# The FFN's first product of a two-layer decoder turned round: tokens as the stationary operand, 32x32 turns on VectorE, transfers within SBUF

## The reference, cut to what matters

```python
D_MODEL, SEQ, DEPTH, CONV_WIDTH = 1024, 256, 2, 3
D_FF = 2816

def conv_ffn(x, w_in, conv_w, conv_b, w_out):     # x (1, 256, 1024), w_in (1024, 5632), w_out (2816, 1024)
    up, gate = jnp.split(x @ w_in, 2, axis=-1)
    up = lax.conv_general_dilated(                 # per feature, over this token and the two before it
        up, conv_w[:, None, :], window_strides=(1,), padding=[(CONV_WIDTH - 1, 0)],
        dimension_numbers=("NWC", "WIO", "NWC"), feature_group_count=up.shape[-1]) + conv_b
    return (jax.nn.gelu(up) * gate) @ w_out

x = layer_norm(DEEPNORM_ALPHA * x + conv_ffn(x, ...), g, b)
```

## Time and profile before

| | us |
|---|---|
| median of three runs | 600.32 (600.27 to 600.74) |
| span of the profiled execution | 598.3 |
| PE busy | 589.4 (99%) |
| DVE busy | 464.9 (78%) |
| ACT busy | 323.7 (54%) |
| POOL busy | 50.5 (8%) |

### The profile page before, as it was taken

How to read it: one execution, slowest core, us unless ns; L and a number is a source line. 1 busy time by engine, 2 the same in 40 slices (tenths; PEclk the granted TensorE clock), 3 DMA queues, 4 the chain that set the end, 5 groups by cost and what they waited for, 6 DMA issues and landing times.

```text
span 598.3 us, 8585 instructions
## 1 busy us (share of the span) xinstructions
PE 589.4 (99%) x3216; PEld 501.1 (84%) x3216; DVE 464.9 (78%) x841; ACT 323.7 (54%) x520; POOL 50.5 (8%) x84
## 2 busy tenths in 40 slices
PE   8999999999999999999999999999999999999995
PEld 6887777898888888889888888889888888888894
DVE  4989994877777778777979797688677777777776
ACT  5756684265445444456445678935554555545430
POOL 6300000300000000000120003132000000000003
PEclk9999999999999999999999999999999999999998
DMA  8996865363556686554457955343755555755601
GB/s 306 296 341 215 261 186 189 139 223 109 184 191 209 211 280 211 192 169 173 172 203 222 302 177 186 108 140 101 251 191 182 188 170 204 242 172 201 210 2 70
DMA packets 82293, 116.38 MB, mean 195 GB/s; under 512 B 11292, under 2 KB 60236, under 8 KB 82252
## 3 DMA queue, kind: packets, MB, share of 16 engines
q1 hardware_dynamic: 80812, 111.64, 56.3%
q0 software_dynamic: 1152, 4.19, 2.1%
q10 hardware_dynamic: 288, 0.00, 0.0%
HBM read 108.23 MB, written 1.05 MB: 183 GB/s over the span
## 4 chain that ended last, share of the span: by engine, by line
PE 98%; DVE 1%; ACT 0%; DVEq 0%; issue 0%
PE wide L1294 18%; PE wide L1295 18%; PE wide L1296 18%; PE score L1501 11%; PE score L1507 6%; PE turn L1501 5%; PE outb L1501 5%; PE outb L1507 3%; PE turn L1507 3%; PE score L1307 1%; PE turn L1393 1%; PE outb L1419 1%; PE score L1296 1%; PE score L1295 1%; PE score L1294 1%; PE wide L1315 1%
## 5 line engine op out<-in xcount | busy, mean ns | idle before, releaser
L965 DVE TENSOR_TENSOR w_lo<-raw,w_hi 128x2048 fp32r<-128x2048 f32 (+1 forms) x120 | 211.0, 1776 | 60.6 <-ACT w_hi L772 60.4
L772 ACT ACTIVATE w_hi<-raw 128x2048 fp32r<-128x2048 f32 (+1 forms) x126 | 182.2, 1483 | 34.5 <-PE wide L1296 23.6
L1294 PE MATMUL wide<-w_hi,xT 128*128 128x512 f32 (+1 forms) x256 | 95.7, 374 | 0.3 <-DVE w_lo L1031 0.2
L1294 PE MATMUL wide<-w_hi,oT_hi 128*128 128x512 f32 x240 | 95.3, 397 | 0.0
L1295 PE MATMUL wide<-w_lo,oT_hi 128*128 128x512 f32 x240 | 93.7, 391 | 0.0
L1296 PE MATMUL wide<-w_hi,oT_lo 128*128 128x512 f32 x240 | 93.6, 390 | 0.0
L1296 PE MATMUL wide<-w_hi,xT 128*128 128x512 f32 (+1 forms) x256 | 93.0, 363 | 0.0
L1295 PE MATMUL wide<-w_lo,xT 128*128 128x512 f32 (+1 forms) x256 | 92.9, 363 | 0.0
L893 ACT ACTIVATE qT<-kT,conv_cols 128x256 f32<-128x256 f32 x36 | 21.7, 602 | 93.1 <-DVE kT L1198 93.1
L1501 PE MATMUL score<-xT,w_hi 128*128 128x512 f32 x288 | 68.3, 389 | 0.0
L1501 PEld LDWEIGHTS score<-xT,w_hi 128*128 128x128 f32 x288 | 53.9, 188 | 11.1
(11 more groups left out here) (182 smaller groups left out, 809.6 us busy)
## 6 DMA issues: line engine op xcount, KB each, us to landing
raw<-in_ffn_w_in SPq DMA_DIRECT2D x44, 1024.0 KB, 5.1
raw<-in_ffn_w_out SPq DMA_DIRECT2D x22, 1024.0 KB, 4.9
raw<-in_a_w_qkv SPq DMA_DIRECT2D x9, 1024.0 KB, 6.1
raw<-in_w_kv_shared SPq DMA_DIRECT2D x8, 1024.0 KB, 5.6
raw<-in_a_w_o SPq DMA_DIRECT2D x4, 1024.0 KB, 6.5
raw<-in_b_w_q SPq DMA_DIRECT2D x4, 1024.0 KB, 5.1
raw<-in_b_w_o SPq DMA_DIRECT2D x4, 1024.0 KB, 5.1
raw<-in_a_w_qkv SPq DMA_DIRECT2D x4, 512.0 KB, 7.7
```

The lines of the kernel that those rows point to most:

```text
L772: ins = nc.scalar.activation(w_hi[c % RING][:, part], raw[c % RAW_RING][:, part], ACT.Copy)
L965: ins = nc.vector.tensor_tensor(w_lo[c % RING][:, part], raw[c % RAW_RING][:, part], w_hi[c % RING][:, part].bitcast(F32), ALU.subtract)
L1294: nc.tensor.matmul(dst, a_hi, b_hi, start=start, stop=False, skip_group_check=True)
```

## The change

The first product holds the tokens stationary in every group: x's high or low part for 128 tokens is loaded, and 512 columns of weights stream past, 256 of `up` and 256 of `gate`. A chunk of `w_in` is now four of the eight row blocks for both, loaded by two transfers. The result has tokens on partitions, in two PSUM banks per group (`in_banks`, two pairs in turn). DVE turns each bank by blocks of 32x32 into `turned` (`turn_in`), SP moves the blocks in four transfers to `in_moved` (`in_move`), which is a part of the tensor `kT`, and ACT copies `up` out of it and applies the middle tap (`taps`). What was added up, copied or turned by TensorE is gone. The second product runs two groups behind, and the hidden tiles have four buffers. The splits of chunks are written ahead of the instructions that wait for a move.

```diff
+HIDDEN = 4
+MOVE_AHEAD = 6
...
         if which == 2:
-            return base + 3 * i + 2 if i == GROUPS - 1 else base + 3 * i + 4
-        return base + 3 * i - 1 + which if i > 0 else base + which
+            return base + (3 * i + 6 if i < GROUPS - 2 else 2 * GROUPS + i)
+        return base + (2 * i if i < 3 else 3 * i - 2) + which
+
+    def second_behind(i):
+
+        return [i - 2] if i >= 2 else []
...
+    for layer in range(LAYERS):
+        for i in range(GROUPS):
+            ffn_moves_ahead[ffn_chunk(layer, i, 1) + MOVE_AHEAD] = (layer, i)
...
+            def in_move(layer, i):
+                t = GROUPS * layer + i
+                sp.wait_ge(in_turned, ST * t + ST)
+                for a in range(4):
+                    sp.dma_start(in_moved[:, a, :], turned[32 * a:32 * a + 32, t % 2, :, :]).then_inc(in_carried, 16)
-            def load(c, dst, src):
+            def load(c, *parts):
+                if c in ffn_moves_ahead:
+                    in_move(*ffn_moves_ahead[c])
...
+                def taps(i):
+
+                    t = GROUPS * layer + i
+                    act.wait_ge(in_carried, 64 * (t + 1))
                     for tt in range(2):
+                        if t > 0:
+                            act.wait_ge(conv_done, 2 * t + tt - 1)
+                        nc.scalar.activation(by_quarters(up[:, tt, :]), carried(tt), ACT.Copy)
+                        nc.scalar.activation(by_quarters(conv[:, tt, :]), carried(tt), ACT.Identity,
...
+                for i in range(GROUPS):
+                    split_hi(ffn_chunk(layer, i, 0) + RING)
+                    if i:
+                        make_h_hi(i - 1)
+                    if i < GROUPS - 1:
+                        split_hi(ffn_chunk(layer, i, 1) + RING)
+                        for n in second_behind(i):
+                            split_hi(ffn_chunk(layer, n, 2) + RING)
+                        taps(i)
+                        make_gelu(i)
+                    else:
+                        split_hi(ffn_chunk(layer, i, 1) + RING, 0)
+                        split_hi(ffn_chunk(layer, i, 1) + RING, 1)
+                        taps(i)
+                        make_gelu(i)
+                        make_h_hi(i)
...
+                def turn_in(i, st):
+
+                    t = GROUPS * layer + i
+                    dve.wait_ge(*((in_rows_done, t + 1) if st == 0 else (chunk_used, ffn_chunk(layer, i, 1) + 1)))
+                    if st == 0 and t >= 2:
+                        dve.wait_ge(in_carried, 64 * (t - 1))
+                    bank = (wide[0:2] if i == 0 else in_banks[(i - 1) % 2])[st]
+                    into = turned[:, t % 2, :, :].rearrange("p b (j s t) -> p b j s t", j=4, s=ST)
+                    nc.vector.transpose(into[:, :, :, st, :], bank[:, :].rearrange("p (j f b) -> p b j f", j=4, b=4)
+                                        ).then_inc(in_turned, 1)
...
+                for i in range(GROUPS):
+                    turn_in(i, 0)
+                    split_lo(ffn_chunk(layer, i, 0) + RING)
+                    turn_in(i, 1)
+                    if i:
+                        for tt in range(2):
+                            make_h_lo(i - 1, tt)
+                    if i < GROUPS - 1:
+                        split_lo(ffn_chunk(layer, i, 1) + RING)
+                        for n in second_behind(i):
+                            split_lo(ffn_chunk(layer, n, 2) + RING)
+                        add_taps(i)
+                        for tt in range(2):
+                            make_hidden(i, tt)
+                    else:
+                        split_lo(ffn_chunk(layer, i, 1) + RING, 0)
+                        split_lo(ffn_chunk(layer, i, 1) + RING, 1)
+                        add_taps(i)
+                        for tt in range(2):
+                            make_hidden(i, tt)
+                            make_h_lo(i, tt)
...
+                def in_product(i):
+
+                    t = GROUPS * layer + i
+                    chunks = [ffn_chunk(layer, i, h) for h in range(2)]
+                    banks = wide[0:2] if i == 0 else in_banks[(i - 1) % 2]
+                    if i >= 3:
+                        pe.wait_ge(in_turned, ST * (t - 2) + ST)
+                    for h, st in ((0, 0), (1, 0), (0, 1), (1, 1)) if i == 0 else ((0, 0), (0, 1), (1, 0), (1, 1)):
+                        c = chunks[h]
+                        for k in range(4):
+                            kt = 4 * h + k
...
+                            if i == 0 and st == 0 and kt in (6, 7):
+                                x_transposes(2 * layer + 1, (kt - 4,))
...
+                            last = product(banks[st][:, :], xT_hi[:, kt, rs], xT_lo[:, kt, rs],
                                            w_hi[c % RING][:, cols], w_lo[c % RING][:, cols], kt == 0, kt == KT - 1)
...
+                for i in range(GROUPS):
+                    in_product(i)
+                    for n in second_behind(i):
                         for st in range(ST):
                             for half in range(2):
-                                last = second_product(ffn_chunk(layer, i - 1, 2) % RING, 0, st, half, start=second)
+                                last = out_product(n, st, half)
                         last.then_inc(chunk_used, 1)
```

More of the change, by code:

```diff
@@ L349, in ffn_chunk, with raw_count @@
         if which == 2:
-            return base + 3 * i + 2 if i == GROUPS - 1 else base + 3 * i + 4
-        return base + 3 * i - 1 + which if i > 0 else base + which
[L353 to L362, removed]
+            return base + (3 * i + 6 if i < GROUPS - 2 else 2 * GROUPS + i)
+        return base + (2 * i if i < 3 else 3 * i - 2) + which
+    def second_behind(i):
+        return [i - 2] if i >= 2 else []
+    IN_CHUNKS = {ffn_chunk(layer, i, h) for layer in range(LAYERS) for i in range(GROUPS) for h in range(2)}
+    def raw_count(c):
+        return sum(32 if n in IN_CHUNKS else 16 for n in range(c % RAW_RING, c + 1, RAW_RING))
+    ffn_moves_ahead = {}
+    for layer in range(LAYERS):
+        for i in range(GROUPS):
+            ffn_moves_ahead[ffn_chunk(layer, i, 1) + MOVE_AHEAD] = (layer, i)
     moves_ahead = {}
@@ L582, in load @@
                 slot = c % RAW_RING
[L583 removed]
+                for into, src in parts:
+                    sp.dma_start(into(raw[slot][:, :]), src).then_inc(raw_in[slot], 16)
             for layer in range(LAYERS):
@@ L915, in ffn_group, with make_h_hi @@
[L915 to L924, removed]
-                ffn_group(GROUPS - 1, "last")
+                def make_h_hi(i):
+                    for tt in range(2):
+                        act.wait_ge(hidden_done, 2 * (GROUPS * layer + i) + tt + 1)
+                        if tt == 0 and i >= HIDDEN:
+                            act.wait_ge(chunk_used, ffn_chunk(layer, i - HIDDEN, 2) + 1)
+                        nc.scalar.activation(hT_hi[i % HIDDEN][:, tt, :], hidden[:, tt, :], ACT.Copy).then_inc(hhi_done, 1)
@@ L1243, in ffn_group @@
-                    if peeled == "last":
-                        make_hidden(0)
-                        split_lo(cu + RING, 1)
-                        make_h_lo(0)
-                        make_hidden(1)
-                        make_h_lo(1)
-                        if cg + RING == SHARED:
-                            split_shared_lo()
-                        return
-                    for tt in range(2):
-                        make_hidden(tt)
-                    if not first:
-                        split_lo(cg + RING)
@@ L1604, in _ @@
                         x_transposes(2 * layer + 2, (0,))
-                    last = second_product(ffn_chunk(layer, i, 2) % RING, int(final), st, half, stop=final)
+                    last = out_product(i, st, half)
                     if (st, half) == (1, 1):
```

287 lines of the change are left out of this document (73 added, 214 removed).

## The result

The changed kernel takes 601.92 us (median of 11 runs, 600.56 to 603.21) against 600.25 (11 runs, 599.84 to 601.01): ratio 1.0029, 95% interval 1.0019 to 1.0038. It is slower by about 1.7 us, where 599.1 was predicted. The time lies inside the range that was given (597.2 to 604.0), on the side of the first rival (601.8 for a fall of the clock in one layer).

What follows compares the result with a forecast made beforehand. TensorE's matmuls were taken to bound the kernel. Per layer 12.4 + 152.4 + 11.3 = 176.1 us against 176.7, 1.2 less in both, so 600.3 - 1.2 = 599.1 us; range 597.2 to 604.0.

Steps and rivals of the forecast that it cites:

- the first rival: Clock falls to 1.2 GHz in the wait before group 10's second product: 601.8 us in one layer, 604.5 both; chance 0.25.
- The price of 0.0130 per start: TensorE's matmuls: each costs 0.0130 us beside its columns, so 256 columns take 0.1199 and 512 take 0.2268.
- Group 0: Start of each layer's FFN: 12.4 us, with TensorE waiting 0.6 for the norm's half row.
- The chain behind T: After T, the end of group 10's first product: turn, moves, copies, taps and low parts take 11.3 us per layer.
- PE's wait: TensorE stands still before group 10's second product, 11.3 - 8.2 = 3.1 us in each layer.
- the unknown costs: Bounds per layer: slower PSUM turns add 0.7 to 1.4, a landing at 6.2 adds 3.5, copies -0.2 to 0.4.
- a wait of about 3 us at full clock, 0.58: Likeliest case, at each layer's end: no clock fall, 599.1 us, bounds 597.7 to 600.4; chance 0.58.
- the stretch: From the FFN's first matmul to group 10's second product: 176.1 us predicted against 176.7 before, per layer.
- The price of a fall: Group 10's second product after a clock fall: 12 matmuls at double price, 2.7 us per layer.
- Late landings: Rival: moves land late at the layer's end or inside groups; 602.5 us, at 6.2 it is 606; chance 0.09.
- A shorter chain: Rival: steps at the layer's end overlap better, wait 1 us shorter per layer, 597.1 us; chance 0.06.
- The gain itself: Whole kernel at full clock: 0.6 us less per layer, 1.2 us in both.

Runs made afterwards that it cites:

- halves: The changed kernel with every 512-column matmul of the first product made as two of 256, output not the reference's; 616.15 us.
- hid: The changed kernel with both of DVE's products with the gate made before the low parts in group 10; 600.00 us.
- cover: The changed kernel with group 7's second product moved behind group 10's first product; 594.90 us.
- fill12: The changed kernel with twelve unused 512-column matmuls in TensorE's wait before group 10's second product; 599.40 us.
- fill6: The changed kernel with six unused 512-column matmuls in TensorE's wait before group 10's second product; 599.14 us.
- cover2: Cover with the next layer's first chunk split ahead of the taps, and both gate products ahead of the low parts; 593.16 us.
- again1: The changed kernel, unedited, profiled in another execution; span 600.2 us.

## Why the prediction was wrong

**The sum was right, to a tenth, as a sum at full clock.** The price of 0.0130 per start held (halves, and the 672 matmuls in 152.32). Group 0 took 12.51 for 12.4, with a wait of 0.50 for 0.6. Nothing was late inside the groups: turns of 0.71 from PSUM for the 0.689 taken from SBUF, moves of 2.50 for 2.60, and PE busy throughout. The chain behind T took 11.28 (11.1 in the second layer) for 11.3, and PE's wait was 2.96 and 2.79 for 3.1. No bound of the unknown costs came into play.

**The step that failed is the choice of the likeliest case: "a wait of about 3 us at full clock, 0.58", against "the clock falls in one layer or both 0.25".** In the sum it is the sentence that what follows the stretch, "group 10's second product and the layer norm, stays as it is and only shifts": the clock behind the wait stood there at nothing, and where it fell that product's 36 matmuls took 9.62 us in place of 7.93. Six of eight waits in four traces brought a fall. The argument against that rival, that the wait and the idle time ahead of the fall at the program's end are equal only to a tenth, carried nothing: hid shows that 2.3 us can be enough, and the first profile that 2.96 need not be. At these lengths the fall comes in one execution and not in another, and a rival that says so had to have well over 0.25. By the rule of the Trainium skill that the prediction cited (TensorE: Matmul & The Clock Gate, Why this matters for your kernels) the fall was the likelier course, and the traces agree with it.

**The price of a fall was taken too high.** "I take 12 of them, 2.7 us": it was 7 or 8 matmuls, 1.7 us. So 1.5 falls make 2.5 us an execution, where both layers were to make 5.4. With the right price and a fall in three waits of four, the same sum would have given 599.1 + 2.5 = 601.6. That the rival's 601.8 for one layer is so near the 601.92 measured is luck: the median execution has two falls, each cheaper.

**Late landings** (0.09) did not come: the moves at the end landed 2.7 to 2.9 us behind their last issue. **A shorter chain** came only by edits (hid, cover). **The gain itself** was 0.9 by fill12 and 1.3 by fill6 for 1.2: right in direction, and as small as forecast, since the wait at the layer's end gives nearly all of it back.

**Two smaller slips.** "The median of the runs lies 2.0 above the span and I carry that over" did not hold: the kernel before lies 1.8 above its span (median of 38 later executions, 1.75 to 1.86), the changed one 2.3 (1.85 to 2.62), and fill12 2.3 as well. So about half a microsecond of the loss lies outside the span, and by spans fill12's gain is 1.4 (597.1 against 598.5). What that half microsecond is stays open. And two thirds of 0.58 are 0.39, not the 0.36 from which the chance of "faster" was added up.

## What to carry to other kernels

A wait of TensorE has two prices: its length, and what the clock does behind it. Where a change opens a wait of a few microseconds on TensorE, add the second price with the chance that the traces of that kernel bear out, and look at the spread of the runs: a median above the profiled execution, with runs some microseconds apart, says that the profile may show a lucky one. When a path becomes longer at the end of a pipeline, first look for work that can be put behind its start (here one group's second product, 7.0 us with cover's edit alone and 8.8 with cover2's), before shortening the path.

## What was not expected of the hardware

- The same wait in the same program brings the fall in one execution and not in the next: none and 8, 8 and 8, none and 8, 7 and 7 slow matmuls in the two layers of four executions. The Trainium skill (TensorE: Matmul & The Clock Gate, Part 1: The HAM clock gate) says that the gate's watching isn't tied to the kernel's start, so that one kernel shows different counts of slow matmuls; the traces agree.
- The fall can come when TensorE has been busy again for 0.5 us (again1) or 1.3 us (hid), at full clock until then. A look at the clock in the wait itself, or at the first matmul behind it, would have missed it.
- Matmuls that feed nothing are worth 2.5 us here, since no fall comes behind a wait that they fill.
